# Gate and up of the feed-forward parts with tokens on the partitions

## The chip, the cores and the metric

One core of a Trainium2 chip runs the whole program in one launch. The metric is the device time of that launch in microseconds (us). Three executions of the kernel before took 1697.83 us in the median (1696.63 to 1698.01).

## The reference, cut to what matters

A model of two layer pairs on 256 tokens of width 1024, in float32: attention mixers and, behind or between them, six gated feed-forward parts of width 2816.

```python
def swiglu(h, w_in, w_out):
    g, u = jnp.split(h @ w_in, 2, axis=-1)
    return (jax.nn.silu(g) * u) @ w_out
```

Two of the six (called ff0 and ff1 here) follow a mixer whose result is joined and layer-normed (with a gain and a bias). The other four (f1a, f2a, f1b, f2b) divide by the root mean square of each token and have separate gate, up and down weights; half of their result is added to the stream.

## The kernel before

**Three products for one.** Every float32 matrix is split into a high part (ScalarE copies it to fp32r, L1447 for weights) and a low part (VectorE subtracts, L1847 for weights), and each product is three matmuls: high by high, high by low, low by high.

**Units.** Weights come in units of 1 MB (128 partitions x 2048 values) through a ring of three slots: SyncE loads one (L1180), ScalarE and VectorE split it, TensorE uses it (`unit_used`), and the slot is free for the next. A chunk of a feed-forward part is 256 of its 2816 features, 11 chunks to a part: one unit of gate, one of up and one of down.

**Feed-forward part (TensorE: `ffn`, L2662).** `cols_unit` (L2382) makes gate and up of a chunk with features on the partitions: the weights are stationary, and the 256 tokens of the normed stream (`hH`, `hL`) move; 48 matmuls of 256 columns for gate into bank 4, as many for up into bank 5. ScalarE applies silu to gate (L1631, L1633), VectorE multiplies by up (L2076), ScalarE and VectorE split the product into `aH` and `aL` (L1625, L2082), and `rows_unit` (L2424) uses it as it lies as the stationary side for down: 24 matmuls of 512 columns, into banks 0 to 3, which hold the sum over all chunks. In the loop the order on TensorE is gate(i), down(i-1), up(i). In the four root-mean-square parts the factor of a token lies along the columns, so it is made into a row, by a product with a diagonal matrix (`row_bc`, L2491), and VectorE multiplies every gate chunk by it (L2070).

**Start of a part.** The stream `x` has tokens on the partitions. TensorE turns it in 16 transposes of 128x128 (`transposed`, L2481), which write both token tiles of two 128-column pieces into one bank; the pieces are scaled out of the banks and split into `hH`, `hL`; the first unit follows the pieces as they come (`tl_ready`). Before ff0, ff1, cd and f1a TensorE runs 12 matmuls on zeros, and 5 more behind the transposes (`keep_busy`, L2465). Ahead of ff0, ff1, cd and f1a stands a layer norm on VectorE and ScalarE (`layer_norm`, `root`), and the gain and bias are put on `x` itself (`affine`, L2160, L2163) behind the splits of the first units. ff0 carries, beside its own work, the conditioning matrix (`ada`, L1865: eight VectorE steps for each 2 MB that GpSimd's queue loads).

**End of a part.** `rows_last` does the last two down units, token tile 0 first; VectorE adds each finished bank to `x` (L2174, or L2132 and on in a layer norm) and the next part's transposes wait for it (`nat_ready`, `x_part`). f1a also turns 40 tiles of weights for the recurrence of the mixer behind it (L2725, L2737) into banks 6 and 7.

Each engine runs its own program in the order written; the order across engines is by semaphores alone.

## Time and profile before

| | |
|---|---|
| median of three executions | 1697.83 us |
| the profiled execution | 1696.68 us, of which the span is 1694.7 us |
| TensorE busy | 1626.8 us (96% of the span), 12192 instructions |
| weight loads of TensorE | 1493.5 us (88%) |
| VectorE busy | 1103.1 us (65%) |
| ScalarE busy | 791.2 us (47%) |
| DMA | 330.20 MB, 195 GB/s |
| TensorE clock granted, mean | 0.991 |

Matmuls overlap in the array, so the duration of one (284 ns for 256 columns, 394 ns for 512) is not the time from one to the next. That one is read where a row of the chain of waits holds many of them, as its length divided by their number.

### The profile page before, as it was taken

To read this page: it belongs to the slowest core of one execution; us is meant where nothing else is said; L and a number is where in the kernel's file an instruction comes from. 1 tells how busy PE (TensorE), PEld (TensorE's weight loads), DVE (VectorE), ACT (ScalarE), POOL (GpSimd) and SP (SyncE) were. 2 spreads that over 40 slices of the span, in tenths; PEclk is the share of its full clock that TensorE was granted. 3 is DMA by queue.
4 is the path that set the end of the run, shared out by engine and by line. 5 is a ranking of instruction groups with operands and counts; after the bars stand their busy time and mean duration, and the time that the engine had idled before them with its cause. 6 is when DMAs were issued, how large, how long until landed. Compare 5 with 4: busy or idle time off the path is not lost.

```text
span 1694.7 us, 29837 instructions
## 1 busy us (share of the span) xinstructions
PE 1626.8 (96%) x12192; PEld 1493.5 (88%) x12199; DVE 1103.1 (65%) x1315; ACT 791.2 (47%) x966; POOL 230.3 (14%) x300
## 2 busy tenths in 40 slices
PE   3999999999999999999999999999999999999999
PEld 2997899978888999889998978999899999889998
DVE  7787878888677444665557886555555556755554
ACT  1564534346455333543446645434544345663433
POOL 2101000000000000078945200000000002200000
PEclk9999999999999999999999999999999999999999
DMA  9975888874646555466554434656465555445552
GB/s 319 335 244 180 281 297 281 297 274 136 234 154 198 175 198 173 149 187 198 173 180 144 151 101 156 198 173 198 149 199 178 193 178 172 142 145 186 185 186 98
DMA packets 221693, 330.20 MB, mean 195 GB/s; under 512 B 6359, under 2 KB 183096, under 8 KB 221614
## 3 DMA queue, kind: packets, MB, share of 16 engines
q1 hardware_dynamic: 206416, 276.91, 50.2%
q0 software_dynamic: 14800, 52.06, 8.9%
q8 instruction: 58, 0.95, 0.2%
q10 hardware_dynamic: 398, 0.11, 0.0%
q14 instruction: 21, 0.17, 0.0%
HBM read 327.97 MB, written 1.09 MB: 194 GB/s over the span
## 4 chain that ended last, share of the span: by engine, by line
PE 76%; DVE 11%; DMA 6%; ACT 3%; issue 3%; SPq 0%; POOLq 0%; DVEq 0%; POOL 0%; ACTq 0%
PE bank L2382 40%; PE bank L2424 22%; PE bank L2412 7%; DMA s_late<-in_w_ada 5%; DVE s_late L1865 4%; DVE s_wL L1847 2%; DMA s_mix<-in_w_ada 1%; PE bank L2394 1%; ACT s_wH L1447 1%; PE bank L2518 1%; PE bank L2481 1%; DVE s_late L1877 1%; DVE s_t L2132 0%; ACT s_mix L1472 0%; PE bank L492 0%
## 5 line engine op out<-in xcount | busy, mean ns | idle before, releaser
L1847 DVE TENSOR_TENSOR s_wL<-s_raw,s_wH 128x2048 fp32r<-128x2048 f32 x254 | 585.0, 2308 | 323.0 <-ACT s_wH L1447 322.0
L2382 PE MATMUL bank<-s_hH,s_wH 128*128 128x256 f32 x2240 | 636.7, 284 | 8.9 <-DVE s_hL L1895 5.2
L2382 PE MATMUL bank<-s_hL,s_wH 128*128 128x256 f32 x2240 | 633.8, 283 | 0.0
L2382 PE MATMUL bank<-s_hH,s_wL 128*128 128x256 f32 x2240 | 633.8, 283 | 0.0
L1447 ACT ACTIVATE s_wH<-s_raw 128x2048 fp32r<-128x2048 f32 x254 | 484.2, 1907 | 175.7 <-PE bank L2424 123.2
L2382 PEld LDWEIGHTS bank<-s_hH,s_wH 128*128 128x128 f32 x2240 | 429.7, 192 | 14.0 <-issue 9.4
L2382 PEld LDWEIGHTS bank<-s_hL,s_wH 128*128 128x128 f32 x2240 | 429.8, 192 | 2.4 <-issue 0.2
L2382 PEld LDWEIGHTS bank<-s_hH,s_wL 128*128 128x128 f32 x2240 | 429.7, 192 | 0.0
L2424 PE MATMUL bank<-s_wH,s_aH 128*128 128x512 f32 x496 | 195.4, 394 | 1.1 <-DVE s_hL L1969 0.9
L2424 PE MATMUL bank<-s_wL,s_aH 128*128 128x512 f32 x496 | 194.3, 392 | 0.0
L2424 PE MATMUL bank<-s_wH,s_aL 128*128 128x512 f32 x496 | 193.6, 390 | 0.0
L1625 ACT ACTIVATE s_aH<-s_mix 128x512 fp32r<-128x512 f32 x60 | 37.9, 631 | 273.4 <-DVE s_mix L2076 273.4
L2424 PEld LDWEIGHTS bank<-s_wH,s_aH 128*128 128x128 f32 x496 | 93.7, 189 | 19.9 <-DVE s_hL L1969 0.9
L2424 PEld LDWEIGHTS bank<-s_wH,s_aL 128*128 128x128 f32 x496 | 93.5, 189 | 20.1
L2424 PEld LDWEIGHTS bank<-s_wL,s_aH 128*128 128x128 f32 x496 | 93.8, 189 | 17.3 <-issue 0.2
L2076 DVE TENSOR_TENSOR s_mix<-s_mix,bank 128x512 f32<-128x512 f32 x66 | 45.3, 686 | 77.7 <-PE bank L2382 77.6
L2412 PE MATMUL bank<-s_hH,s_wH 128*128 128x256 f32 x288 | 84.6, 294 | 4.4 <-DVE s_hL L1882 4.4
L1631 ACT ACTIVATE s_mix<-s_mix 128x512 f32<-128x512 f32 x44 | 27.9, 633 | 128.8 <-DVE s_mix L2070 128.7
L1865 DVE SCALAR_TENSOR_TENSOR s_late<-s_late,s_silc 128x512 f32<-128x512 f32 x94 | 70.7, 752 | 18.1 <-DMA s_late<-in_w_ada 15.1
L2412 PE MATMUL bank<-s_hL,s_wH 128*128 128x256 f32 x288 | 82.2, 285 | 0.0
L2412 PE MATMUL bank<-s_hH,s_wL 128*128 128x256 f32 x288 | 82.2, 285 | 0.0
L2082 DVE TENSOR_TENSOR s_aL<-s_mix,s_aH 128x512 fp32r<-128x512 f32 x60 | 42.2, 703 | 42.2 <-ACT s_aH L1625 42.2
(451 smaller groups left out, 2014.1 us busy)
## 6 DMA issues: line engine op xcount, KB each, us to landing
s_raw<-in_w_ffn_in SPq DMA_DIRECT2D x44, 1024.0 KB, 5.9
s_raw<-in_ffn_w_gate SPq DMA_DIRECT2D x44, 1024.0 KB, 5.3
s_raw<-in_ffn_w_up SPq DMA_DIRECT2D x44, 1024.0 KB, 5.3
s_raw<-in_ffn_w_down SPq DMA_DIRECT2D x44, 1024.0 KB, 4.9
s_late<-in_w_ada POOLq DMA_DIRECT2D x20, 2048.0 KB, 10.1
s_raw<-in_w_ffn_out SPq DMA_DIRECT2D x22, 1024.0 KB, 5.1
s_raw<-in_w_in_ab SPq DMA_DIRECT2D x12, 1024.0 KB, 10.1
s_raw<-in_w_in_cd SPq DMA_DIRECT2D x12, 1024.0 KB, 6.1
```

Source lines behind the costliest of these rows:

```text
L1447: A(wH[:, slot, :], raw[:, slot, :], ACT.Copy).then_inc(hi_ready, 1)
L1625: A(aH[:], act.rearrange("p (a t) -> p a t", a=2), ACT.Copy).then_inc(act_hi, 1)
L1631: A(sil, gsc, ACT.Silu).then_inc(sil_done, 1)
L1847: TTn(wL[:, slot, :], raw[:, slot, :], wH[:, slot, :].bitcast(F32), ALU.subtract).then_inc(lo_ready, 1)
L1865: STT(acc, src, silc[:, k:k + 1], rows_b if k == 0 else acc, ALU.mult, ALU.add)\
L1877: STT(acc, ada_raw[:, slot, 512 * k:512 * k + 512], silc[:, k:k + 1], ada_b[:, slot, :] if k == 0 else acc, ALU.mult, ALU.add).then_inc(ad ...
L2076: TTn(act, sil, bank[5][:], ALU.mult).then_inc(act_mul, 1)
L2082: TTn(aL[:], halves(act), aH[:].bitcast(F32), ALU.subtract).then_inc(act_lo, 1)
L2382: last = mm(dst[:, ft * T:ft * T + T], w, h[:, k, :], start=opens(name, ft, k, i), stop=(k == KC - 1 and i == 2), skip_group_check=True)
L2394: last = mm(dst[:, tt * UC:tt * UC + UC], h, w[:, k, :], start=opens(name, tt, k, i), stop=(k == KC - 1 and i == 2), skip_group_check=True)
L2412: last = mm(dst[:, out_c], w, z, start=opens(name, half, k, i), stop=(k == KC - 1 and i == 2), skip_group_check=True)
L2424: last = mm(bank[SUM_BANK[name][2 * tt + h] if name else 2 * tt + h][:], s, w[:, k, c], start=(start and k == 0 and i == 0), stop=(stop an ...
```

## The change

Gate and up are made with tokens on the partitions. A unit is now half of the input features of gate and up together (4 x 128 input features, 256 gate columns beside 256 up columns), and `half_unit` holds a token tile of `hH` or `hL` stationary while 512 weight columns move: 12 matmuls of 512 columns for each half and token tile, both halves into one bank per token tile (4 and 5). Silu and product are done for each token tile of 128x256, the factor of the token enters as a per-partition scale, and the product is turned by four transposes into bank 6 (`turn_act`) before it is split. The order in the loop on TensorE is lower half, upper half, down(i-1), turning(i). `row_bc` and the multiplication by the row are gone from the feed-forward parts. The input is turned and split by token tile (`turn_tile`, `normed`, `rms_pieces`), tile 0 of the next part inside the last down unit where no layer norm stands between. The first run of filler matmuls is 4 instead of 12 before ff0, ff1 and f1a. Every unit is loaded by two DMAs. The steps of `ada` at the end of ff0 are spread, and f1a turns its weights four at a time through bank 7. Of the diff, the kept and the added lines of the new functions are shown; the lines that they replace stand in the kernel above.

```diff
+                     else (4, 5, 6, 7) for n in TR}
+        GU_BANK, ACT_BANK = (4, 5), 6
         SUM_BANK = {n: (4, 5, 6, 7) if n in ("o_ab", "o_cd") else (0, 1, 4, 5) if n == "o_even" else (0, 1, 2, 3) for n in SUMS}
         O_BANK = (4, 5, 0, 1)
+        BUSY = {"ff0": (4, 5), "cd": (12, 5), "ff1": (4, 5), "f1a": (4, 5), "even": (0, 6)}
         BUSY_BANK = {n: 4 if n in ("ff0", "ff1") else 0 for n in TR}
...
@@ SyncE @@
+                dst, half = raw[:, slot, :].rearrange("p (k c) -> p k c", k=src.shape[1]), src.shape[1] // 2
+                for k in (0, half):
+                    sp.dma_start(dst[:, k:k + half, :], src[:, k:k + half, :]).then_inc(raw_full[slot], 16)
...
+                def gate_up(slot, n, half, c0):
+                    sp.wait_ge(lo_ready, n + (LO0 - RING + 1))
+                    dst = raw[:, slot, :].rearrange("p (k c) -> p k c", c=2 * UC)
+                    for at, w, first in ((0, wg, g0), (UC, wu, u0)):
+                        src = w[D // 2 * half:D // 2 * half + D // 2, bass.ds(c0 + first, UC)].rearrange("(k p) c -> p k c", p=P)
+                        sp.dma_start(dst[:, :, at:at + UC], src).then_inc(raw_full[slot], 16)
...
@@ ScalarE @@
+                def silu(i, tt):
+                    if tt == 0:
+                        act_e.wait_ge(gu_ready, i + (f + 1))
                     else:
+                        act_e.wait_ge(unit_used, i * 3 + (n0 + USED0 + 1) if not isinstance(i, int) or i else n0 + USED0 + 2)
+                    if name in RFFN and isinstance(i, int) and i == 0:
+                        act_e.wait_ge(diag_ready, 2 * RMS[name] + tt + 1)
+                    A(sil[:, tt, :], bank[GU_BANK[tt]][:, 0:UC], ACT.Silu, scale=rstd[:, tt:tt + 1] if name in RFFN else 1.0)\
+                        .then_inc(sil_done, 1)
+                def hidden(i, dst):
+                    act_e.wait_ge(act_tr, i + (f + 1))
+                    A(dst, bank[ACT_BANK][:].rearrange("p (a t) -> p a t", a=2), ACT.Copy).then_inc(act_hi, 1)
+                silu(0, 0)
+                split_py(n0 + 3)
+                silu(0, 1)
                 split_py(n0 + 4)
+                hidden(0, aH[:])
...
+                    n = i * 3 + (n0 + 2)
+                    split((n0 + 2) % RING, n, i + ((n0 + 2) // RING + 1))
+                    if drive:
+                        drive(0)
+                    silu(i, 0)
+                    if drive:
+                        drive(1)
+                    silu(i, 1)
+                    split((n0 + 3) % RING, n + 1, i + ((n0 + 3) // RING + 1))
+                    if drive:
+                        drive(2)
+                    hidden(i, aH[:])
+                    split((n0 + 4) % RING, n + 2, i + ((n0 + 4) // RING + 1))
...
+            def normed_piece(name, e, tt, half):
+                g = 2 * tt + half
+                act_e.wait_ge(tr_done, TRD[name] + g + 1)
+                for k in range(4):
+                    c = 4 * half + k
+                    last = A(tF[:, c, tt * P:tt * P + P], bank[TURN_BANK[name][g]][:, k * P:k * P + P], ACT.Identity,
+                             scale=lnS[:, e, c:c + 1], bias=lnS[:, e, 8 + c:9 + c])
+                last.then_inc(t32_odd, 1)
+                act_e.wait_ge(t32_odd, T32_ODD[name] + g + 1)
+                upper_piece(tt, half)
+            def upper_piece(tt, half):
+                c, t = slice(4 * half, 4 * half + 4), slice(tt * P, tt * P + P)
+                A(hH[:, c, t], tF[:, c, t], ACT.Copy).then_inc(th_ready, 1)
+            def normed(name, e):
+                root(e, 0)
+                split_py(START[name] + 1)
+                normed_piece(name, e, 0, 0)
+                root(e, 1)
+                normed_piece(name, e, 0, 1)
+                normed_piece(name, e, 1, 0)
+                normed_piece(name, e, 1, 1)
+                split_py(START[name] + 2)
...
@@ VectorE @@
+                def product(i, tt):
+                    dve.wait_ge(sil_done, i * 2 + (2 * f + tt + 1))
+                    up = bank[GU_BANK[tt]][:, UC:2 * UC]
                     if name in RFFN:
+                        STT(act[:, tt, :], up, rstd[:, tt:tt + 1], sil[:, tt, :], ALU.mult, ALU.mult).then_inc(act_mul, 1)
+                    else:
+                        TTn(act[:, tt, :], up, sil[:, tt, :], ALU.mult).then_inc(act_mul, 1)
+                def hidden(i, high, low):
                     dve.wait_ge(act_hi, i + (f + 1))
+                    TTn(low, bank[ACT_BANK][:].rearrange("p (a t) -> p a t", a=2), high.bitcast(F32), ALU.subtract).then_inc(act_lo, 1)
+                product(0, 0)
                 split_py(n0 + 3)
+                product(0, 1)
                 split_py(n0 + 4)
+                hidden(0, aH[:], aL[:])
...
+                    n = i * 3 + (n0 + 2)
+                    split((n0 + 2) % RING, n)
+                    product(i, 0)
+                    product(i, 1)
+                    split((n0 + 3) % RING, n + 1)
+                    hidden(i, aH[:], aL[:])
+                    split((n0 + 4) % RING, n + 2)
...
+                    with dve.Fori(0, 7) as b:
+                        ada(1, b + 6)
+                        body(b + 1)
+                    ada(1, 13)
+                    ada_some(0, 4, 0, 4)
+                    body(8)
+                    ada_some(0, 4, 4, 8)
                     body(9)
+                    ada_some(0, 5, 0, 4)
...
+            def rms_pieces(y, name, gain):
+                residual_half(y, 0, 0)
+                residual_half(y, 0, 1).then_inc(nat_ready, 1)
+                rms_piece(name, 0, 0, gain)
+                rms_piece(name, 0, 1, gain)
+                residual_half(y, 1, 0).then_inc(x_part, 1)
+                lower_piece(name, 0, 0)
+                residual_half(y, 1, 1).then_inc(nat_ready, 1)
+                lower_piece(name, 0, 1)
+                row_scale(name, 0)
+                split_py(START[name] + 1)
+                rms_piece(name, 1, 0, gain)
+                rms_piece(name, 1, 1, gain)
+                lower_piece(name, 1, 0)
+                lower_piece(name, 1, 1)
+                row_scale(name, 1)
+                split_py(START[name] + 2)
...
+                layer_norm(e, gate, y, name)
                 split_py(START[name] + 1)
+                lower_piece(name, 0, 1)
+                if name == "f1a":
+                    affine(e, 0)
+                lower_piece(name, 1, 0)
+                lower_piece(name, 1, 1)
+                if name != "f1a":
                     split_py(START[name] + 2)
+                    affine(e, 0)
+                affine(e, 1)
+                if name == "f1a":
+                    row_scale(name, 0)
+                    row_scale(name, 1)
+                    split_py(START[name] + 2)
...
@@ TensorE @@
+            def turn_tile(name, tt):
+                if tt and name in XPART:
+                    pe.wait_ge(x_part, XPART[name] + 1)
+                else:
+                    pe.wait_ge(nat_ready, 2 * TR[name] + tt + 1)
+                for k in range(KC):
+                    if name in FFN:
+                        b, at = 2 * tt + k // 4, (k % 4) * P
+                    else:
+                        b, at = k // 2, (k % 2) * T + tt * P
+                    if tt and k == 4 and name in XPART:
+                        pe.wait_ge(nat_ready, 2 * TR[name] + 2)
+                    last = pe.transpose(bank[TURN_BANK[name][b]][:, at:at + P], x[:, tt, k * P:k * P + P], ident[:])
+                    if k % 4 == 3 if name in FFN else tt and k % 2:
+                        last.then_inc(tr_done, 1)
...
+            def ffn(name, after=None, with_ada=False):
+                n0, f, ready = START[name], 11 * FFN[name], 4 * TR[name]
+                def half_unit(slot, half, tt):
+                    H, L = (w[:, slot, :].rearrange("p (k c) -> p k c", k=4) for w in (wH, wL))
+                    for k in range(4):
+                        c, t = 4 * half + k, slice(tt * P, tt * P + P)
+                        for i, (h, w) in enumerate(((hH[:, c, t], H), (hH[:, c, t], L), (hL[:, c, t], H))):
+                            last = mm(bank[GU_BANK[tt]][:], h, w[:, k, :], start=(half == 0 and k == 0 and i == 0),
+                                      stop=(half == 1 and k == 3 and i == 2), skip_group_check=True)
+                    if tt == 1:
+                        last.then_inc(unit_used, 1)
+                    elif half == 1:
+                        last.then_inc(gu_ready, 1)
+                def turn_act(i):
+                    pe.wait_ge(act_mul, i * 2 + (2 * f + 2))
+                    for tt in range(TT):
+                        for ft in range(2):
+                            last = pe.transpose(bank[ACT_BANK][:, ft * T + tt * P:ft * T + tt * P + P], act[:, tt, ft * P:ft * P + P], ident[:])
+                    last.then_inc(act_tr, 1)
+                def lower_half(slot, n, i, weights=None):
+                    pe.wait_ge(lo_ready, n + (LO0 + 1))
+                    pe.wait_ge(act_mul, i * 2 + (2 * f - 1))
+                    half_unit(slot, 0, 0)
+                    if weights:
+                        weights(0)
+                    pe.wait_ge(act_mul, i * 2 + 2 * f)
+                    half_unit(slot, 0, 1)
+                    if weights:
+                        weights(1)
+                def upper_half(slot, n, weights=None):
+                    pe.wait_ge(lo_ready, n + (LO0 + 1))
+                    half_unit(slot, 1, 0)
+                    if weights:
+                        weights(0)
+                    half_unit(slot, 1, 1)
+                    if weights:
+                        weights(1)
+                def body(i, first=False, weights=(None, None, None)):
                     n = i * 3 + (n0 - 1)
+                    lower_half((n0 + 2) % RING, n, i, weights[0])
+                    if first:
+                        turn_act(0)
+                    upper_half((n0 + 3) % RING, n + 1, weights[1])
                     pe.wait_ge(act_lo, i + f)
+                    rows_unit((n0 + 4) % RING, n + 2, aH, aL, 0, first)
+                    if weights[2]:
+                        weights[2](0)
+                    turn_act(i)
...
+                if name not in XPART:
+                    keep_busy(TURN_BANK[name][0], BUSY[name][0])
+                    turn_tile(name, 0)
+                    keep_busy(BUSY_BANK[name], BUSY[name][1])
+                pe.wait_ge(lo_ready, n0 + (LO0 + 1))
+                pe.wait_ge(tl_ready, ready + 1)
+                half_unit(n0 % RING, 0, 0)
+                turn_tile(name, 1)
+                pe.wait_ge(lo_ready, n0 + (LO0 + 2))
+                pe.wait_ge(tl_ready, ready + 2)
+                half_unit((n0 + 1) % RING, 1, 0)
+                pe.wait_ge(tl_ready, ready + 3)
+                half_unit(n0 % RING, 0, 1)
+                pe.wait_ge(tl_ready, ready + 4)
+                half_unit((n0 + 1) % RING, 1, 1)
+                body(1, first=True)
                 if with_ada:
...
                 elif name == "f1a":
                     with pe.Fori(2, FC - 2) as i:
                         body(i)
+                    body(FC - 2, weights=(output_weights, drive_weights, lambda h: drive_weights(2)))
                 else:
                     with pe.Fori(2, FC - 1) as i:
                         body(i)
+                last = name == "f1a"
+                lower_half((n0 + 29) % RING, n0 + 29, FC - 1, (lambda h: drive_weights(3 + h)) if last else None)
+                upper_half((n0 + 30) % RING, n0 + 30, (lambda h: drive_weights(5 + h)) if last else None)
+                a_slot, b_slot = (n0 + 31) % RING, (n0 + 32) % RING
+                pe.wait_ge(lo_ready, n0 + 31 + (LO0 + 1))
                 pe.wait_ge(act_lo, FC - 1 + f)
+                rows_half(a_slot, aH, aL, 0, 0, False, False, None, (0,))
+                if last:
+                    drive_weights(7)
+                turn_act(FC - 1)
+                rows_half(a_slot, aH, aL, 0, 0, False, False, None, (1,))
+                rows_half(a_slot, aH, aL, 0, 1, False, False, None, (0,))
+                pe.wait_ge(lo_ready, n0 + 32 + (LO0 + 1))
+                pe.wait_ge(act_lo, FC + f)
+                rows_half(b_slot, hH, hL, 0, 0, False, True, None, (0,))
                 if with_ada:
```

## Rows read from the trace of the kernel before

**Rows 1.** The page: shares of the chain that ended last, by line.
```profile
PE bank L2382 40%; PE bank L2424 22%; PE bank L2412 7%; DMA s_late<-in_w_ada 5%; DVE s_late L1865 4%; DVE s_wL L1847 2%; DMA s_mix<-in_w_ada 1%; PE bank L2394 1%; ACT s_wH L1447 1%; PE bank L2518 1%; PE bank L2481 1%; DVE s_late L1877 1%; DVE s_t L2132 0%; ACT s_mix L1472 0%; PE bank L492 0%
```

**Rows 2.** Chain of waits in order of time: start us, length us, what; inside f2a.
```profile
1058.30 11.51 PE bank L2382 x96
1069.81 5.47 PE bank L2424 x24
```

**Rows 3.** Groups of the page: the weight splits, and the `ada` steps.
```profile
L1847 DVE TENSOR_TENSOR s_wL<-s_raw,s_wH 128x2048 fp32r<-128x2048 f32 x254 | 585.0, 2308 | 323.0 <-ACT s_wH L1447 322.0
...
L1447 ACT ACTIVATE s_wH<-s_raw 128x2048 fp32r<-128x2048 f32 x254 | 484.2, 1907 | 175.7 <-PE bank L2424 123.2
...
L1865 DVE SCALAR_TENSOR_TENSOR s_late<-s_late,s_silc 128x512 f32<-128x512 f32 x94 | 70.7, 752 | 18.1 <-DMA s_late<-in_w_ada 15.1
```

**Rows 4.** Timeline of TensorE (start us, us, instruction): transposes between matmuls.
```profile
502.22 0.39 PE L2424 MATMUL bank<-s_wH,s_hL 128*128 128x512 f32 x1
502.45 0.60 PE L2534 MATMUL bank<-s_ident,s_mix 128*128 128x128 f32 x4
502.89 0.38 PE L2537 MATMUL bank<-s_ident,s_mix 128*128 128x128 f32 x2
503.02 0.48 PE L2424 MATMUL bank<-s_wH,s_hH 128*128 128x512 f32 x1
503.34 0.40 PE L2424 MATMUL bank<-s_wL,s_hH 128*128 128x512 f32 x1
...
881.92 1.03 PE L2737 MATMUL bank<-s_ident,s_late 128*128 128x128 f32 x8
882.71 0.36 PE L2382 MATMUL bank<-s_hH,s_wH 128*128 128x256 f32 x1
```

**Rows 5.** Groups by line and shape: busy us, mean ns of one | idle before, releaser.
```profile
L1472 ACT ACTIVATE s_mix<-s_mix,s_small 128x128 f32<-128x128 f32 x40 | 15.8, 396 | 26.7 <-DVE s_small L1933 26.6
...
L1465 ACT ACTIVATE s_hH<-s_t 128x512 fp32r<-128x512 f32 x28 | 16.3, 625 | 5.8 <-DVE s_t L768 3.8 <-DVE s_t L1911 1.2 <-DVE s_t L901 0.5
...
L1882 DVE TENSOR_TENSOR s_hL<-s_t,s_hH 128x512 fp32r<-128x512 f32 x28 | 18.8, 688 | 5.7 <-ACT s_hH L1465 4.9
```

**Rows 6.** Chain in order of time, from f2a to f1b.
```profile
1211.41 10.92 PE bank L2424 x48
...
1225.35 5.99 PE bank L2382 x48
1231.34 0.45 PE bank L2491 x4
1231.78 11.52 PE bank L2382 x96
```

**Rows 7.** Timeline of TensorE: last down matmul before ff1; fillers before f1a.
```profile
513.03 0.39 PE L2424 MATMUL bank<-s_wH,s_hL 128*128 128x512 f32 x1
...
710.73 2.54 PE L2465 MATMUL bank<-s_zeros 128*128 128x512 bf16 x11
```

**Rows 8.** Timeline of ScalarE and VectorE at the start of ff1.
```profile
516.64 0.29 ACT L1729 ACTIVATE s_small<-s_small 128x1 f32<-128x1 f32 x1
...
518.26 0.81 DVE L2138 TENSOR_SCALAR s_x<-s_x,s_small 128x1024 f32<-128x1024 f32 x1
...
530.73 2.35 DVE L2160 TENSOR_TENSOR s_x<-s_x,s_mix 128x1024 f32<-128x1024 f32 x2
```

**Rows 9.** Chain in order of time: first units of ff1, first loop unit of f1a.
```profile
523.85 17.32 PE bank L2382 x144
...
733.01 6.02 PE bank L2382 x48
```

**Rows 10.** Chain in order of time: the last load of the conditioning matrix in ff0.
```profile
345.30 12.41 DMA s_late<-in_w_ada
```

**Rows 11.** Windows: stretch, us, TensorE busy (x), granted clock, DMA share, GB/s.
```profile
175.50:178.70 3.20, 3.20 (x13) 0.51 1.03 391
520.20:523.40 3.20, 3.20 (x13) 0.51 0.00 0
```

479 lines of the change are left out of this document (192 added, 287 removed).

## The prediction, made blind

> **What bounds the kernel now.** I read the chain of waits first, by line. TensorE's three big lines alone hold 69% of the span: L2382 (gate and up, features on partitions), L2424 (down), L2412 (mixers) [rows 1]. Then the chain in order of time: inside a feed-forward part it is two alternating rows and nothing between them, 96 matmuls of gate and up in 11.51 us, 24 of down in 5.47 us, 16.98 us to a chunk [rows 2]. So TensorE never waits there, and what counts in the six parts is the time that its own instructions take and the gaps at the ends. The other engines are full for about half of such a period: three weight splits take VectorE 3 x 2.31 = 6.9 us and ScalarE 3 x 1.91 = 5.7 us [rows 3]. The sum below is made on the profiled execution, 1696.68 us, which lies 1.15 us under the median.
>
> **The loop, 66 chunks.** A matmul that moves 256 columns takes 11.51/96 = 0.1199 us of TensorE, one that moves 512 takes 5.47/24 = 0.2279 us [rows 2]. Gate and up become 48 of the latter: 10.94 us, 0.57 us less. The new work is four transposes a chunk. Six transposes between down matmuls took 503.02 - 502.45 = 0.57 us, and the first matmul behind them 0.32 us instead of 0.228, so 0.66 us in all; eight took 882.71 - 881.92 = 0.79 us without that second term, some 0.87 us with it [rows 4]. That is 0.10 us each and 0.07 us fixed, so four cost 0.47 us. Bounds: 0.40 us (fixed part hidden) and 0.66 us (as six). Net gain 0.10 us a chunk, 6.6 us over 66, with bounds of 11 us gained and 6 us lost.
>
> The Trainium skill, "TensorE: Matmul & The Clock Gate", section "Back-to-back issue gap", gives an isolated matmul its columns over 2.4 GHz plus 2.5 ns, which would leave gate and up at 10.36 us against 10.48 us before: 0.12 us saved, less than the transposes cost, and the whole sum some 30 us worse. The trace does not agree: two matmuls of 256 columns cost 12 ns more than one of 512 columns [rows 2].
>
> New waits in the loop. `turn_act(i)` waits for the product of tile 1, and behind it stands all of TensorE. Silu and product of a 128x256 tile take some 0.4 us each (bounds 0.2 us, half of a 128x128 piece, and 0.63 us, a 128x512 piece [rows 5]); neither engine has a split in front of them in its queue then, and the 5.47 us of down stand between. Covered by 4 us. `lower_half` waits for the products because gate and up of a tile share a bank: in the loop they are some 5 us early. `hidden` comes behind the turning and has the next 10.94 us. In ff0, VectorE carries eight `ada` steps of 0.75 us a chunk as well [rows 3], so 6.0 + 6.9 + about 1.7 for products and low part, 15 us of a period of some 17.8, and its products end about 2.5 us behind the upper half: still covered.
>
> Gone are the multiplication by the row and half of the weight loads; both lay beside other work and are worth nothing. SyncE issues two DMAs of 512 KB where it issued one of 1 MB, and the gate and up pieces keep their runs of 1 KB; no load of a unit is on the chain [rows 1]. Nothing, with 0 to +2 us as bounds (ff0's conditioning loads share the DMA engines). GpSimd's start of f1a's weights waits for an earlier event; its end is waited for ten chunks later. Nothing.
>
> **Starts behind a root mean square (f2a, f1b, f2b).** Before: down ends at 1211.41 + 10.92 = 1222.33 us, the third unit at 1231.78 + 11.52 = 1243.30 us [rows 6]. That is 20.97 us for 17.27 us of matmuls: 3.7 us over (3.0 us from the last down matmul to the first unit, of which the 16 transposes are some 1.8 by the price above, `row_bc` 0.45, small gaps the rest). After: transposes of tile 0 stand in the last down unit (their `nat_ready` comes 0.4 us before they do), about 1.0 us; then a wait of 0.25 us, because VectorE has the add of tile 1, half 0, ahead of the first low piece; tile 1's transposes 1.0 us; and about 0.3 us until the split of the second unit, behind five small operations and `row_scale`. Sum 2.6 us, a gain of 1.1 us each, 3.3 us. Bounds 0 and 2 us each. The mixers even and odd get their tile 0 transposes early too: 0.5 us each, 1.0 us (bounds 0 and 1).
>
> **Starts behind a layer norm.** In ff1 down ends at 513.26 us [rows 7]. The deviation of tile 0 is there at 516.93 us, but `x` tile 0 is normalised only from 518.26 us [rows 8], behind tile 1's statistics. Moved ahead it ends at 517.9 us; transposes to 518.9; ScalarE's first piece, four 128x128 operations (0.35 us each, after the 0.40 of L1472) and a 128x512 copy (0.6 us), ends at 520.8, its low part (0.7 us) at 521.5 [rows 5]. First half unit at 521.5 us, where it was 523.85 us [rows 9]. Then it turns. Gate and up share a bank, so the fifth half unit (`lower_half(1)`) must wait for `product(0, 0)`, and that stands on VectorE behind the splits of units 1 and 2 and both `affine` (2.35 us a pair, two pairs [rows 8]). VectorE: low piece 3 until 529.3, split until 532.8 (ScalarE gives it at 530.5), affine until 537.4, product until 537.9. TensorE has done its four tile halves at 533.6 and idles 4.3 us. It ends the work of three units at 543.4 us; before that was 523.85 + 17.32 = 541.2 us [rows 9], with 0.86 us more of matmuls in it. So the start of ff1 loses 3.1 us beyond the loop's gain, and that of ff0 3.0 us in the same way. Before, only gate's silu was waited for, so `affine` cost nothing.
>
> f1a has `affine` too, and the squares behind it. Before: down ended at about 710.7 us, the third unit at 733.01 + 6.02 = 739.0 us [rows 7, 9]. After, one `affine` lies between low pieces; the last root is there at 727.8, split until 730.1, product 730.6, third unit's work done at 736.0: 3.0 us earlier, 2.1 us of it beyond the loop. Bounds for these three starts together: from -9 to +2 us; I take -4.0.
>
> **Ends.** In ff0 the last 2 MB for `ada` land after 12.4 us, at 357.7 us [rows 10]; eight steps follow on VectorE with the last gate unit, its split and product behind them. With the previous steps halved that load starts about 3 us earlier, and half of the steps move behind the products: 3.1 us gained (0 to 5). In f1a the ten insertions of four transposes cost 0.35 us more than five of eight, and `hidden` of the last chunk waits behind one split: 0.5 us. Together -0.9 us. The cd norm is 0.35 us later by its new order (in the 3.1 us).
>
> **The clock.** In 3.2 us at the starts of ff0 and ff1 the granted clock was 0.51, so the level of 1.2 GHz, after TensorE had idled nearly 4 and 3 us; transposes and fillers stood there, so it cost about 1 us each [rows 11]. After, the first idle time is no shorter (4 fillers for 12), and half units follow sooner; and the new 4.3 us of idle time ahead of `lower_half(1)` would be followed by such a stretch in dense matmuls, where 3.2 us at half clock lose 1.6 us. I put 1.6 x 2 + 0.45 x 2 = 4.1 us, bounds 0 and 8.
>
> **Sum.** +6.6 +3.3 +1.0 -3.1 -3.0 +2.1 +3.1 -0.9 -4.1 = 5.0 us gained: 1691.7 us in the profiled execution's terms, 1692.8 us as a median.
>
> **Rivals.**
> 1. *The turning is not 0.47 us* (slower). If each `turn_act` costs what six transposes did, 0.66 us, or waits 0.2 us for its product, 66 x 0.19 = 12.5 us are lost: 1705.5 us. It decides from 0.54 us a chunk on. For it: after transposes the next matmuls are late [rows 4]. Against: the six and the eight agree on 0.10 us each. By the skill's rule named above it would be slower yet. Chance 0.16.
> 2. *Starts cost more* (no change). The wait for `product(0, 0)` and the slow stretches reach f1a as well, or the second unit's split is later: 4 us more, 1697 us. For it: VectorE is the longest queue at every start. Against: f1a has its splits behind the roots, not before. Chance 0.19.
> 3. *No price at the starts.* The clock stays up and the early end of ff0 is kept: 4 to 5 us better, 1688.5 us. For it: a stretch of 1.2 GHz did not follow every wait (none at f1a). Chance 0.17.
> The forecast holds 0.48.
>
> **Numbers.** A measurement here tells 0.2%, 3.4 us, from no change: faster is under 1694.4 us. The forecast's own range is 1689.5 to 1696 us; a quarter of its cases lie above 1694.4. Faster: 0.36 + 0.17 + 0.03 = 0.56; same: 0.12 + 0.13 = 0.25; slower: 0.16 + 0.03 = 0.19. For 8 in 10 the range reaches over rivals 2 and 3 and part of the first: 1686 to 1701.5 us.
>
> **What the changed profile would show.** Loop: rows of 48 matmuls of 512 columns in 10.9 us, a `turn_act` of about 0.5 us with no releaser named, 16.9 us a chunk. If a VectorE product is named as releaser, rival 1. Starts of ff0 and ff1: TensorE idle some 4 us with VectorE's product as releaser and L2160-like adds ahead of it; idle time at f1a about 3 us. f1b: three units' work done about 18 us behind the last down matmul. Clock: stretches at 0.5 behind these waits. I am wrong if the chunk is over 17 us, if no such wait is there, or if the end of ff0 is not earlier.

## The result, and the profile after

The changed kernel takes 1700.9 us (median of 20 runs, 1696.3 to 1706.9), the kernel before 1695.4 us in the runs beside it: ratio 1.0034, 95% interval [1.0025, 1.0042]. The forecast was 1692.8 us and faster. It is slower by 0.34%, inside the range given but on the wrong side.

The profiled execution took 1701.27 us (before: 1696.68 us), its span 1699.3 us at a mean granted clock of 0.984 (before: 1694.7 us, 0.991). From its page, the busy shares and the chain by line, which answers to [rows 1]; L2756 is gate and up, L2504 down, L2768 the turning of the product:

```profile
PE 1619.1 (95%) x9255; PEld 1352.6 (80%) x9255; DVE 1078.7 (63%) x1313; ACT 814.3 (48%) x1052; POOL 224.8 (13%) x300
PE 78%; DVE 10%; DMA 6%; ACT 4%; issue 2%; SPq 0%; POOLq 0%; DVEq 0%; POOL 0%; ACTq 0%
PE bank L2756 37%; PE bank L2504 22%; PE bank L2492 7%; DMA s_late<-in_w_ada 5%; DVE s_late L1902 4%; PE bank L2462 3%; DVE s_wL L1884 2%; PE bank L2768 2%; DMA s_mix<-in_w_ada 1%; PE bank L2474 1%; ACT s_wH L1456 1%; PE bank L2603 1%; DVE s_late L1914 1%; PE bank L2559 1%; ACT s_mix L1741 1%
```

The loop did what it was changed for. The chain in order of time inside f2a (start, length, what), the answer to [rows 2]:

```profile
1171.39 5.44 PE bank L2504 x24
1176.83 0.44 PE bank L2768 x4
1177.27 10.93 PE bank L2756 x48
1188.20 5.44 PE bank L2504 x24
...
1194.08 10.91 PE bank L2756 x48
```

A chunk is 1188.20 - 1171.39 = 16.81 us, where it was 16.98 us [rows 2]: 0.18 us gained in a chunk, some 12 us over 66. All of this was given back, and more, between the loops. At the start of ff1 the chain leaves TensorE; the answer to [rows 9]:

```profile
538.21 1.91 ACT s_wH L1456
...
542.36 1.23 DVE s_x L2196
543.61 1.23 DVE s_x L2197
544.84 1.15 DVE s_x L2196
546.00 1.24 DVE s_x L2197
...
547.38 0.43 DVE s_mix L2107
...
547.95 7.31 PE bank L2756 x24
```

VectorE splits a weight unit (in the rows left out), runs both `affine` (L2196, L2197), and only then `product(0, 0)` (L2107), for which the fifth half unit waits. The waits of TensorE (line waited for, us in total, times, longest) show two such waits, one at ff0 and one at ff1, and a shorter one at f1a (L2105):

```profile
PE bank L2756 <- DVE s_mix L2107: 10.4, 2, 5.2
PE bank L2756 <- DVE s_mix L2105: 2.9, 1, 2.9
PE bank L2768 <- DVE s_mix L2107: 1.5, 2, 1.2
```

The last matmuls of that chain piece are slow as well: 24 of them in 7.31 us are 0.30 us each, not 0.228. Windows of TensorE (stretch, length, busy time by engine, granted clock, DMA share, GB/s) show why, at ff0, in ff0's chunk 8, ahead of cd, at f1a and at ff1:

```profile
193.20:196.60 3.40, 3.40 (x9) 2.68 (x10) 3.40 (x3) 0.00 (x0) 0.00 (x0) 0.54 0.06 13
340.00:343.40 3.40, 3.40 (x10) 2.59 (x9) 3.02 (x3) 0.52 (x2) 0.00 (x0) 0.54 1.08 357
387.90:391.30 3.40, 2.55 (x10) 2.00 (x11) 1.79 (x3) 2.94 (x4) 0.00 (x0) 0.50 0.00 0
746.30:749.70 3.40, 3.40 (x11) 2.64 (x10) 3.40 (x3) 1.78 (x1) 3.40 (x8) 0.56 1.03 323
548.00:551.40 3.40, 3.40 (x8) 2.71 (x9) 3.40 (x3) 0.00 (x0) 0.63 (x2) 0.51 0.77 243
```

Each of the five lies just behind an idle stretch of TensorE, and in each the engine ran at its level of 1.2 GHz. Four hold dense matmuls (at ff0, ff1 and f1a 24 of them took 7.3 us instead of 5.6). The one ahead of cd begins in transposes and fillers and lasts into cd's first projection, whose first 48 matmuls took 7.0 us, where the kernel before took 6.0. Not every wait is followed so: two waits of 1.6 us at f1a's transposes, and two of 1.5 and 1.8 us in the mixer even, are not.

By stretches of the two timelines, "after" minus "before" (the same work on both sides; the loop's own gain of 0.86 us in a start's three units of work is taken out of the starts and put with the loops):

| stretch | forecast, gain | measured, gain |
|---|---|---|
| loops with their tails | +6.6 | +11.2 |
| starts of f2a, f1b, f2b, mixers even and odd, end of f1a | +3.4 | +2.4 |
| starts of ff0 and ff1, with the clock | -3.0 -3.1 -4.1 | -6.7 -6.3 |
| start of f1a | +2.1 | -1.5 |
| end of ff0 and start of cd | +3.1 | -4.1 |
| first mixer, cd and its end | 0 | +0.4 |
| sum | +5.0 | -4.6 |

### The profile page after: what moved, and what is told of

It is laid out like the page before. It is cut to its first block, busy times and chain, and to the rows that moved or that the text cites. A ratio compares the mean times of both kernels' runs of the same rounds, so it can differ in the third digit from the quotient of the medians.

```text
span 1699.3 us, 24692 instructions
## 1 busy us (share of the span) xinstructions
PE 1619.1 (95%) x9255; PEld 1352.6 (80%) x9255; DVE 1078.7 (63%) x1313; ACT 814.3 (48%) x1052; POOL 224.8 (13%) x300
## 4 chain that ended last, share of the span: by engine, by line
PE 78%; DVE 10%; DMA 6%; ACT 4%; issue 2%; SPq 0%; POOLq 0%; DVEq 0%; POOL 0%; ACTq 0%
PE bank L2756 37%; PE bank L2504 22%; PE bank L2492 7%; DMA s_late<-in_w_ada 5%; DVE s_late L1902 4%; PE bank L2462 3%; DVE s_wL L1884 2%; PE bank L2768 2%; DMA s_mix<-in_w_ada 1%; PE bank L2474 1%; ACT s_wH L1456 1%; PE bank L2603 1%; DVE s_late L1914 1%; PE bank L2559 1%; ACT s_mix L1741 1%
## 5 line engine op out<-in xcount | busy, mean ns | idle before, releaser
L2756 PE MATMUL bank<-s_wH,s_hH 128*128 128x512 f32 x1056 | 422.5, 400 | 16.2 <-DVE s_mix L2107 10.4
L2756 PE MATMUL bank<-s_wH,s_hL 128*128 128x512 f32 x1056 | 414.3, 392 | 0.0
L2756 PE MATMUL bank<-s_wL,s_hH 128*128 128x512 f32 x1056 | 413.9, 392 | 0.0
L2756 PEld LDWEIGHTS bank<-s_wH,s_hH 128*128 128x128 f32 x1056 | 200.1, 189 | 61.0 <-issue 17.4
L2756 PEld LDWEIGHTS bank<-s_wH,s_hL 128*128 128x128 f32 x1056 | 199.7, 189 | 43.1
L2756 PEld LDWEIGHTS bank<-s_wL,s_hH 128*128 128x128 f32 x1056 | 200.4, 190 | 39.8 <-issue 0.2
L2504 PE MATMUL bank<-s_wH,s_aH 128*128 128x512 f32 x496 | 194.3, 392 | 1.1 <-DVE s_hL L2006 0.9
L2504 PE MATMUL bank<-s_wH,s_aL 128*128 128x512 f32 x496 | 193.3, 390 | 0.0
L2504 PE MATMUL bank<-s_wL,s_aH 128*128 128x512 f32 x496 | 193.0, 389 | 0.0
L2504 PEld LDWEIGHTS bank<-s_wH,s_aH 128*128 128x128 f32 x496 | 93.1, 188 | 20.9 <-DVE s_hL L2006 0.9
L2504 PEld LDWEIGHTS bank<-s_wH,s_aL 128*128 128x128 f32 x496 | 93.1, 188 | 19.6
L2504 PEld LDWEIGHTS bank<-s_wL,s_aH 128*128 128x128 f32 x496 | 93.1, 188 | 19.0
L2492 PE MATMUL bank<-s_hH,s_wH 128*128 128x256 f32 x288 | 85.4, 297 | 3.4 <-DVE s_hL L1919 3.4
L2492 PE MATMUL bank<-s_hL,s_wH 128*128 128x256 f32 x288 | 82.8, 287 | 0.0
L2492 PE MATMUL bank<-s_hH,s_wL 128*128 128x256 f32 x288 | 82.6, 287 | 0.0
L2105 DVE SCALAR_TENSOR_TENSOR s_mix<-bank,s_small,s_mix 128x256 f32<-128x256 f32 x88 | 42.3, 481 | 49.9 <-ACT s_mix L1640 49.9
```

Source lines behind the costliest of these rows:

```text
L2105: STT(act[:, tt, :], up, rstd[:, tt:tt + 1], sil[:, tt, :], ALU.mult, ALU.mult).then_inc(act_mul, 1)
L2492: last = mm(dst[:, out_c], w, z, start=opens(name, half, k, i), stop=(k == KC - 1 and i == 2), skip_group_check=True)
L2504: last = mm(bank[SUM_BANK[name][2 * tt + h] if name else 2 * tt + h][:], s, w[:, k, c], start=(start and k == 0 and i == 0), stop=(stop an ...
L2756: last = mm(bank[GU_BANK[tt]][:], h, w[:, k, :], start=(half == 0 and k == 0 and i == 0), stop=(half == 1 and k == 3 and i == 2), skip_gro ...
```

## The experiments

All ratios are to the kernel before, from runs beside it on the same chip; there were three such sets, on three chips. Theory: the loss is at the starts behind a layer norm and at the end of ff0, in orders of VectorE's queue. Rivals: it is in the loop; or it is chance of the clock.

**The changed kernel again.** 

> The changed kernel as it is, beside the three others on the same chip: 0.3% above the kernel before, 1701 us, as every theory has it.

Measured: 1.0039 [1.0026, 1.0052]. The same as at first. Its profiled execution ran 8.5 us longer than the first one, in places: 2.2 us before ff0's first chunk was turned, 3.7 us in ff0's chunks and 2.7 us at ff1's start, where half units behind the first transposes took 0.43 us a matmul too. In that trace the granted clock was 0.50 for some 6.8 us around each of these places, twice as long as at most of them in the first. So where TensorE has idled, the stretches at 1.2 GHz differ from run to run, and a single trace is good to some 8 us of the total; below, the traces are read piece by piece.

**`affine` behind the products.**

```
 normed:    split_py(START[name] + 2)
-           affine(e, 0)
-           affine(e, 1)           # ff0 and ff1
 ffn:       hidden(0, aH[:], aL[:])
+           affine(e, 0); affine(e, 1)
```

> Edit: in ff0 and ff1 VectorE's four layer-norm adds and multiplies on the residual (1.22 us each, 4.9 us) are issued behind the first chunk's products and its hidden split, not ahead of product(0,0). Theory (the changed kernel loses at the starts, where the fifth half unit waits for product(0,0) behind them): the 36 matmuls that took 13.71 us take 9.5 us or less, at ff0 and ff1; the 24 matmuls behind them at 0.30 us each are at 0.228 where the wait is short enough; 8.5 to 13 us less than the changed kernel, 1688 to 1692 us. Rival 1 (the loss is in the loop, by turning or loading): no change, 1701 us. Rival 2 (VectorE has no room in ff0's first chunks beside the conditioning rows): the time comes back in ff0's chunks 1 to 3, only ff1 gains, 1694 to 1697 us.

(At f1a nothing is moved.) Measured: 1695.1 us, 0.9989 [0.9977, 1.0002], 0.45% under the changed kernel. From the first of the 36 matmuls to the fifth half unit it was 8.7 us instead of 13.7, wait included, at both starts. From the last down matmul to ff1's first turning it was 27.3 us and not 33.3 (36.0 in the repeat). At ff0 5.4 us were gained too, and more than that, 8.4 us, was lost in the next two chunks (16.8 and 20.7 us, where the changed kernel had 11.4 and 17.7). The timeline of TensorE and the chain at that place:

```profile
212.82 1.12 PE L2770 MATMUL bank<-s_ident,s_mix 128*128 128x128 f32 x4 [5.23 <-DVE s_mix L2107]
```

```profile
197.94 1.23 DVE s_x L2199
...
201.59 1.24 DVE s_x L2200
...
203.63 0.77 DVE s_late L1902
...
209.15 0.76 DVE s_late L1902
...
211.27 10.45 DMA s_late<-in_w_ada
```

The second turning waited 5.23 us for its product: `affine` now stood in front of the eight conditioning steps, and these in front of the product. Rival 2 of this run, for ff0; the theory, for ff1. The loop as the place of the loss is out.

**`affine` spread.** The layer norm's edit as before; in ff0 the loop's first two turns on VectorE are written out, with one tile's `affine` behind each:

```
-                    with dve.Fori(0, 7) as b:
+                    for tt in range(TT):
+                        ada(1, tt + 6)
+                        body(tt + 1)
+                        affine(0, tt)
+                    with dve.Fori(2, 7) as b:
```

> Edit: as in the run with the layer-norm operations behind the first chunk's hidden split, but in ff0 tile 0's two stand behind chunk 1 and tile 1's two behind chunk 2, where VectorE waited up to 3.1 us for the DMA of the conditioning rows. Theory (the loss at both starts is the product's place behind them, and in ff0 it was given back because VectorE had no room in chunk 0): ff0 keeps its gain of 4 to 6 us, ff1 keeps 7 to 8 us, 11 to 14 us less than the changed kernel, 1687 to 1690 us. Rival (in ff0 VectorE is the bound wherever they stand): as the run before, 1694 to 1696 us.

Measured: 1689.6 us, 0.9963 [0.9949, 0.9977], 0.7% under the changed kernel, some 12 us, and now faster than the kernel before. Start of ff0 28.1 us (34.2 and 35.1 in the two traces of the changed kernel), start of ff1 29.1 us (33.3 and 36.0), and ff0's next chunk 11.4 us as there; the two chunks behind it took 0.7 us more than in the first trace and as much as in the second. No wait for the product of ff0 or ff1 is left among TensorE's longest. The two starts make 10.3 of the 12.6 us between the two profiled executions; 1.6 us in ff0's chunk 9 and 0.8 us at f1a are places where the clock did not fall this time, in neither of which anything was edited. Even so the place of four VectorE instructions at each of two starts is worth more than the whole loss of 5.8 us.

**Conditioning rows behind chunk 8.**

```
-                    ada_some(0, 4, 0, 4)
                     body(8)
-                    ada_some(0, 4, 4, 8)
+                    ada(0, 4)
                     body(9)
```

> Edit: near the end of ff0 VectorE's eight steps of the conditioning rows (0,4) (6.2 us) are issued whole behind chunk 8, not four ahead of it and four behind it. Theory: TensorE's wait of 1.4 us in chunk 8's turning goes, and the 3.4 us at 1.2 GHz behind it (1.6 us); 3 us less than the changed kernel, 1698 us. Rival (the wait only moves: chunk 9's gate rows wait for VectorE): the same wait stands in chunk 9, 1701 us or 1 us more. If the loss is in the loop: no change.

Measured: 1703.4 us, 1.0035 [1.0023, 1.0046]: no gain. Chunk 7 to 8 fell from 19.1 to 17.7 us, but 8 to 9 took 20.8 us (20.3 before the edit). The chain there:

```profile
343.96 7.03 PE bank L2755 x31
350.99 1.96 issue
352.95 1.10 PE bank L2533 x2
```

The gate matmul of these rows (L2533) stands in the middle of chunk 9's gate and up, and VectorE's eight steps ended at 352.85 us. The wait had moved, as the rival said; the granted clock did not fall behind it in this trace. So the matmul was moved too:

```
-                    body(9, weights=(None, gate_rows, None))
+                    body(9, weights=(None, None, gate_rows))
 ...        # and ScalarE's copy of its result one step later
```

> Edit: VectorE's conditioning rows (0,4) whole behind chunk 8, and TensorE's gate matmul of them (with ScalarE's copy) behind chunk 9's down rows, not in the middle of its gate and up. Theory (in the run before the wait of 1.96 us only moved to the gate matmul): chunks 7 to 8 and 8 to 9 take 17.7 and 18.2 us instead of 19.1 and 20.3 us, 3 to 4 us less than the changed kernel, 1697 us. Rival (the waits are filled by others): less than 1 us, 1700 us.

Measured: 1700.8 us, 1.0018 [1.0008, 1.0028]. The chain of the same chunks:

```profile
341.87 11.01 PE bank L2755 x48
352.89 5.44 PE bank L2503 x24
358.33 0.86 PE bank L2533 x2
359.19 0.44 PE bank L2767 x4
359.62 10.92 PE bank L2755 x48
```

17.7 and 18.5 us, 3.1 us less than in the changed kernel, with a granted clock of 1.00 from 340.0 to 343.4 us, where it was 0.54. The total moved by 2.7 us, but the two intervals overlap; the trace decides here, not the ratio. And the trace shows what was to be had: in four other runs with the old order (both `affine` runs, the fillers in the wait, cd's old order) the clock did not fall in chunk 9, and 8 to 9 took 18.7 us, not 20.3. Of the 3.1 us, 1.4 are then the wait, 1.6 a fall of the clock that did not come in every run, and 0.1 the gate matmul's new place.

**The clock by itself.** Fillers in the wait for the product, which stays:

```
                 half_unit((n0 + 1) % RING, 1, 1)
+                keep_busy(0, {"ff0": 18, "ff1": 18, "f1a": 12}.get(name, 0))
                 body(1, first=True)
```

> Edit: 18 filler matmuls (12 at f1a) on TensorE behind the fourth half unit of ff0, ff1 and f1a, in the wait for product(0,0), which itself is unchanged. Theory (the wait costs twice: its own length and 3.4 us at 1.2 GHz behind it): the 24 matmuls behind the wait take 5.6 us, not 7.3 us, at the three places, 4 to 5 us less than the changed kernel, 1696 us. Rival (the clock falls there whatever TensorE does, or fillers run over into the real work): 0 to 2 us more. If the loss is the wait alone, no change, 1701 us.

Measured: 1699.8 us, 1.0021 [1.0010, 1.0031]. Windows on the matmuls behind the wait, ff0 and ff1:

```profile
195.00:198.40 3.40, 3.40 (x15) 2.81 (x16) 3.40 (x3) 0.00 (x0) 0.00 (x0) 1.00 0.05 10
548.40:551.80 3.40, 3.40 (x15) 2.81 (x16) 3.40 (x3) 0.00 (x0) 0.63 (x2) 1.00 0.75 241
```

The wait is as long as it was (36 matmuls end and 5.2 us pass until the fifth half unit, of which the fillers leave 1.3 us idle), but the clock is 1.00 behind it, and 24 matmuls take 5.55 us, not 7.3. So the wait's second price, 1.7 us each, is real and comes from idleness: without fillers in it, a wait of 5.2 us was followed by half clock each of the 17 times that it stands in nine traces. At f1a the clock did not fall either, but there three traces without fillers have no fall (below), so f1a shows nothing. In total 2.2 us came of it, with intervals that overlap, where 4 to 5 were expected: at ff1 the half units behind the first transposes ran at 1.2 GHz in this trace, as in the repeat.

> Edit: 12 filler matmuls ahead of tile 0's transposes at ff0, ff1 and f1a, as the kernel before had, not 4. Theory (every new idle stretch of TensorE is followed by about 3.4 us at 1.2 GHz): the stretches at 1.2 GHz at the three starts (6.8 us at ff0 and ff1 together with what follows) get about half as long, 2 to 5 us less than the changed kernel, 1696 to 1699 us. Rival (fillers are themselves work of TensorE that delays tile 0's transposes): 0 to 4 us more. If the mean granted clock is mere chance of a run: no change.

The edit is `BUSY` with 12 for 4 in its first places. Measured: 1701.2 us, 1.0026 [1.0017, 1.0036]: no difference that these intervals tell. The 12 fillers lay wholly in the wait for the transposes (5.44 and 4.85 us, as long as with four), so they cost nothing; the rival of an overrun is out, and the gain expected isn't there. The trace shows why. Windows on ff0's first transposes and on the matmuls behind the wait for the product:

```profile
169.00:175.80 6.80, 2.58 (x15) 1.32 (x14) 4.71 (x11) 6.60 (x15) 1.24 (x2) 1.00 0.98 343
193.60:197.00 3.40, 3.40 (x9) 2.63 (x9) 3.40 (x3) 0.00 (x0) 0.00 (x0) 0.50 0.16 33
```

With 12 fillers the clock stayed at 1.00 around the first transposes of ff0 and of ff1, where all eleven traces with four fillers have a stretch at half clock at both. But the stretch behind the wait for the product was then 6.8 us long at both, as in some runs with four, and its 24 matmuls took 7.9 and 8.1 us, not 7.3: the stretch had gone from transposes and fillers, and got longer in dense matmuls. Whether the second follows from the first is not shown by one trace.

**cd's layer norm in the old order.**

```
-                    if h:
+                    if h and first:        # cd: normalise(0) behind the statistics of tile 1
                         normalise(0)
 ...
                 if first:
                     lower_piece(first, 0, 0)
+                else:
+                    normalise(0)
                 normalise(1)
```

> Edit: ahead of cd the layer norm finishes tile 1's sums and variance before it normalises tile 0, as the kernel before had it; ff0, ff1 and f1a keep the new order. Theory (the new order waits for tile 0's standard deviation and holds tile 1 back): tile 1 is normalised 8.7 us after the first gated piece instead of 9.7 us, cd's first projection starts 1 us earlier, 1 to 2.5 us less than the changed kernel, 1699.5 us. Rival (tile 0's transposes come later by as much): no change, 1701 us.

Measured: 1699.6 us, 1.0014 [1.0005, 1.0023]. From ff0's last down matmul to cd's first projection it was 10.1 us (10.7 in the changed kernel, 8.8 in the kernel before). Both the run's trace and the changed kernel's hold a stretch at half clock there, so they can't price the order. Traces without one there can: 10.2 us with the new order (in the runs with 12 fillers and with the late gate matmul) and 9.2 us with the old one (in the run with all mends, below). The order is worth 1.0 us, as the theory had it, and the fall of the clock 0.5 to 0.9 us; the rest of the 3.4 us in the ratio is not explained by it.

**Tile 0's sum first.**

```
                 rows_half(a_slot, aH, aL, 0, 0, ..., (1,))
-                rows_half(a_slot, aH, aL, 0, 1, ..., (0,))
                 ...        # b_slot, tile 0, both halves
+                rows_half(a_slot, aH, aL, 0, 1, ..., (0,))
                 rows_half(a_slot, aH, aL, 0, 1, ..., (1,))
```

> Edit: at the end of all six feed-forward parts both down units are summed for tile 0 before tile 1's first quarter, so that tile 0's sum is whole 5.5 us before the end and not 4.1 us. Theory (the forecast's step at f1a failed by this order): at ff1 and f1a tile 0's transposes start 1 us or more nearer to the last down matmul, while TensorE waits about 0.6 us in the tail for the last hidden product; 0 to 3 us less than the changed kernel, 1698 to 1701 us. Rival (the wait for the hidden product, six times 1 us or more, outweighs it): 2 to 5 us more, 1703 to 1706 us.

Measured: 1709.6 us, 1.0066 [1.0050, 1.0081], worse than the rival had it. From the last turning to the last down matmul the six tails are 0.4 to 1.4 us longer than in the changed kernel in five of them and 3.0 us in f1a's, where TensorE waits 2.0 us and its clock falls behind it: 6.8 us in all. The start of cd gets shorter, 8.9 us (10.7, or 10.2 at full clock): there the sum was what tile 0 waited for. But the transposes of tile 0 at f1a come 2.68 us behind the last down matmul, as in the changed kernel (2.67), so there an earlier sum by itself does nothing. VectorE's timeline at that place (last down matmul at 728.5 us) shows what holds them in this run:

```profile
724.01 1.23 DVE L2177 SCALAR_TENSOR_TENSOR s_x<-s_x,s_t 128x1024 f32<-128x1024 f32 x1
727.36 0.69 DVE L2165 TENSOR_TENSOR s_t<-bank,s_gate 128x512 f32<-128x512 f32 x1 [2.13 <-PE bank L2504]
728.09 0.69 DVE L2183 SCALAR_TENSOR_TENSOR s_x<-s_x,s_t 128x512 f32<-128x512 f32 x1
728.81 0.69 DVE L2184 BATCH_NORM_STATS2 s_small<-s_x 128x6 f32<-128x512 f32 x1
729.42 0.67 DVE L2165 TENSOR_TENSOR s_t<-bank,s_gate 128x512 f32<-128x512 f32 x1
730.13 0.16 DVE L2169 RECIPROCAL s_small<-s_small 128x1 f32<-128x1 f32 x1
730.33 0.81 DVE L2171 TENSOR_SCALAR s_x<-s_x,s_small 128x1024 f32<-128x1024 f32 x1
```

`normalise(0)` (L2169, L2171) stands behind four operations on tile 1, the first of which waits for tile 1's own sum. An earlier sum of tile 0 only makes VectorE idle longer, 2.13 us. In the changed kernel itself the two come close together: ScalarE has tile 0's deviation 1.1 us behind the last down matmul (723.6 us), and the queue holds its use up by 0.5 us more.

```profile
724.47 0.29 ACT L1733 ACTIVATE s_small<-s_small 128x1 f32<-128x1 f32 x1
725.22 0.16 DVE L2169 RECIPROCAL s_small<-s_small 128x1 f32<-128x1 f32 x1
```

To bring the transposes forward, sum and queue would both have to change; no run did that. (ff1 follows a mixer, not a feed-forward part, so this edit can't reach its start, and it was as before, 4.87 and 4.86 us.)

**The turning twice.**

```
-                    for tt in range(TT):
+                    for tt in (0, 1, 0, 1):
```

> Edit: TensorE makes the four transposes of each product twice (66 chunks). Theory (the turning costs its own 0.43 us and hides its latency): 66 times 0.40 to 0.44 us, 26 to 29 us more than the changed kernel, 1728 us. Rival of the forecast (the way from the last product through TensorE, ScalarE and VectorE to the down rows is what the chunk waits for): more than 35 us, as the wait is lengthened on every engine of that way.

Measured: 1727.1 us, 1.0178 [1.0162, 1.0195], 1.44% or 24 us over the changed kernel. The chain inside f2a:

```profile
1099.46 5.44 PE bank L2504 x24
1104.90 0.87 PE bank L2768 x8
1105.78 10.90 PE bank L2756 x48
1116.67 5.45 PE bank L2504 x24
```

Eight take 0.87 us, four 0.44 us. The chunk grows from 16.8 to 17.2 us, which makes some 28 us over 66, 4 us over what the ratio gives; that is about as far as the two intervals reach. The rival's 35 us and more are out, and TensorE's own time is all that the turning costs.

**The mends together.** The spread `affine`, the late rows with the late gate matmul, cd's old order, and at f1a one more:

```
                     row_scale(name, 0)
-                    row_scale(name, 1)
                     split_py(START[name] + 2)
+                    row_scale(name, 1)
```

Then the same with more fillers (`BUSY` of 20 and 10, cd 15, 8 and 7, and 3, 3 and 8 in the waits).

> Edit: the spread layer-norm operations, the late conditioning rows and gate matmul, and cd's old layer-norm order together, and at f1a VectorE's split for the fifth half unit issued between the two reciprocals of the RMS scale, not behind both. Theory (the losses stand at separate places and add up): 12, 3 and 3 us of the three runs and 1 us at f1a, 17 to 19 us less than the changed kernel, ratio to the kernel before 0.992 to 0.994, 1683 to 1687 us. Rival (they share one slack, or cd's gain was chance of the clock): 13 us less, 1688 to 1690 us.

Measured: 1684.0 us, 0.9924 [0.9911, 0.9938]. 1.1% under the changed kernel, 18.6 us of the 17 to 19 expected. Between the two profiled executions (17.4 us of span) the places can be read: 5.8 and 5.2 us at the starts of ff0 and ff1, 3.1 us in ff0's chunks 7 to 9, 1.5 us at cd's start, 0.5 us at f1a. Separate savings, and they add up, but for f1a's, which was not run alone and gave half of the 1 us expected. Some of it is clock: in this trace it did not fall at cd.

> Edit: the four mends and more filler matmuls in the waits left: 20 ahead of and 10 behind tile 0's transposes at ff0 and ff1 (10 and 10 at f1a), 15, 8 and 7 around cd's, and 3, 3 and 8 behind the fourth half unit. Theory (waits are followed by 1.2 GHz): mean granted clock of 0.993 or more, half units behind tile 0's transposes in 2.85 us and not 4.3 to 5.2 us at ff0 and ff1, 3 to 6 us less than the four mends alone, 1679 to 1683 us. Rival (fillers run over into the real work): 0 to 3 us more than the mends alone.

Measured: 1683.7 us, 0.9914 [0.9901, 0.9928]. The starts of ff0, ff1 and f1a are 0.6, 0.9 and 0.3 us shorter than with the mends alone, and cd's is 1.7 us longer, because eight fillers stand between tile 0's transposes and tile 1's, which could have followed at once: there the rival holds. The mean clock is 0.993 in both traces, and hides what the fillers did. The trace with the mends alone has 6.8, 6.8 and 3.4 us at half clock at the three starts; with the fillers there is none, and the half units behind tile 0's transposes took 3.0 us, at full clock. In their place that trace has 17 us at half clock at the start of the program, which no edit touched and where the other's profile shows none. By the ratios the fillers gained 1.7 us, with intervals that overlap: less than the 3 to 6 us expected is likely, but 3 is not excluded. Both versions beat both kernels.

## Why the prediction was wrong, point by point

Forecast and measurement lie 9.6 us apart in the profiled execution's terms: 5.0 us gained against 4.6 us lost. The end of ff0 and the start of cd hold 7.2 us of that, the start of f1a 3.6 us, the starts of ff0 and ff1 2.8 us; the loop came out 4.6 us better than forecast.

- **The loop: right, and too small.** 0.10 us a chunk was forecast, 0.18 came. The 48 matmuls cost 10.92 us (10.94 forecast), down 5.44 us (5.47), the turning 0.44 us (0.47): three terms that each erred to the same side. The turning was over-priced mostly by rounding: [rows 4] give (0.87 - 0.66)/2 = 0.105 us for one transpose and 0.03 us fixed, so 0.45 us for four, not 0.10, 0.07 and 0.47; and two points on a line can't "agree" on its slope, as the text against rival 1 has it. No product was waited for in the loops of the five parts without conditioning rows. Rival 1 is refuted, by the rows and by the doubled turning.
- **Starts of ff0 and ff1: the mechanism right, its length short.** The wait was put at 4.3 us and was 5.2 us; `affine` stood where I had put it. With the slow stretch behind it, and the slow half units behind the first transposes, the two starts lost 13.0 us, not 10.2. The spread `affine` shows that it was this: it gave 10.3 us of them back.
- **Starts behind a root mean square and the mixers: two misses that nearly cancel.** f2a, f1b and f2b gained 1.7, 1.6 and 1.1 us in the traces, 4.4 us where 3.3 were forecast. The mixers even and odd, put at +1.0 us together, lost 1.1 us, nearly all of it in even. With -0.7 us at the end of f1a the row comes within 1.0 us of its forecast by luck.
- **The clock: right in kind.** 1.6 us behind a wait in dense matmuls was the term; the traces show 1.6 to 1.7 us, and the fillers in the wait show that idleness is what it follows. It was applied to two places. There were five, and f1a's and chunk 8's are not there in every run.
- **Start of f1a: wrong.** A gain of 2.1 us was forecast, 1.5 us were lost. The step that failed is the date of the last root, "there at 727.8": 17.1 us behind the last down matmul, where the kernel before had 18.6 us. It came 18.7 us behind, no earlier than before, and the product 21.5 us behind, where the working had 19.9; from root to product it was 2.8 us, as forecast. The root waits for the way through tile 0's and tile 1's transposes, and those of tile 0 came only 0.7 us earlier than before (2.7 us behind the last down matmul, not 3.4): `normalise(0)` was moved ahead of tile 1's last addition only, and still stands behind three operations on tile 1 and `gated(1, 1)`, which needs the last down matmuls. Then the clock fell. Where it did not (the repeat and two more traces), this start took 27.95 us, not 28.8, so the fall cost 0.9 us net: behind slow matmuls the second product was no longer waited for, which is 0.4 us where the clock stays up. What holds the root is read from the traces; no run moved `normalise(0)`, and how much it would give stays open.
- **End of ff0: wrong, and the largest miss, 7.2 us.** "With the previous steps halved that load starts about 3 us earlier ... 3.1 us gained" looked at the last conditioning rows alone. Halving them put four of their steps behind the eight of the row before, twelve in a row, ahead of chunk 8's split and product. I had worked out 15 us of VectorE in a chunk of 17.8 for eight steps and called it covered, and did not do the sum for twelve: 15 + 3.1 us is over the chunk. TensorE waited 1.4 us, its clock fell (1.6 us, in four of nine traces with this order), and in chunk 9 the gate matmul took its share. The run with rows and gate late gives 3.1 us of it back. What was claimed did come in part: the wait of 1.65 us for the last rows, which the kernel before has at 362.4 us, is gone. The rest of the loss is at cd's start: 10.7 us from the last down matmul to the first projection, 8.8 before. There the term "0.35 us later by its new order" was mis-sized, as the order cost 1.0 us, and the clock fell too. The prediction's own sign, "if the end of ff0 is not earlier", is what came.
- **Rivals.** The result lies between rival 2 (1697 us) and rival 1 (1705.5 us), and by its mechanism it is rival 2, "starts cost more": a wait and a slow stretch did reach f1a. Its price of 4 us was too low, as it left ff0's end at a gain.

## What to carry to other kernels

A change that saves 0.18 us in each of 66 turns of a loop is paid for, or not, in the few places between loops: write out the queue of every engine there, instruction by instruction, and add it up wherever an edit puts two batches of work behind each other. Operations that nobody waits for (here `affine`) become a cost the moment that a wait is added behind them in the same queue, and where they go must itself be read from the trace: behind the product was right in ff1 and wrong in ff0, whose queue was full for the next two chunks. When a wait is found, price it twice, once for itself and once for the matmuls behind it at half clock; a filler in the wait shows which part is which. And before a mend is credited with a saving, look whether the clock fell at that place in the other traces: half of the 3.1 us of the late rows was that.

## What the runs showed of the hardware that was not expected

- Waits of TensorE could be followed by some 3.4 us at a granted clock of 0.50 to 0.56, and in some runs by twice that (in the repeat, 24 matmuls at ff1 took 8.1 us). It came behind all 17 unfilled waits of 5.2 us in the traces, behind 7 of 10 of the 2.9 us at f1a, and behind 4 of 7 of the 1.3 to 2.1 us in ff0's chunk 8; the same place of the same kernel has it in one run and not in another (f1a, in the first trace and not in the repeat). Of the changed kernel's 20 runs the fastest took 1696.3 us, at a mean clock of 0.991, and the slowest 1706.9 us, at 0.980; over all 20 the mean clock goes with about half of the scatter (correlation -0.69).
- 18 fillers of 512 columns in a wait of 5.2 us, 1.3 us of it left idle, kept the clock at 1.00 for the matmuls behind it at both ff0 and ff1. Ahead of the first transposes 12 instead of 4 kept it at 1.00 there in the one trace of that run, but made no difference in the time that could be measured.
- Four fp32 transposes of 128x128 took 0.44 us and eight 0.87 us, 0.11 us each with no fixed part. The reading of [rows 4] had a part of 0.07 us for each group, of which 0.04 was rounding.
